# A decoder step in three-term float32: GpSimd splits one half chunk of weights at each hand-over, and four weight tiles start from the first x tile

## What is computed

```python
x = x + 0.5 * rms_norm(swiglu(rms_norm(x, ng[0]), ffn1_gate[l], ffn1_up[l], ffn1_down[l]), ng[1])
mix, s, cg, cs = mixer(rms_norm(x, ng[2]), cache_gdn_conv[l], cache_sconv[l], state_gdn[l], segments, ...)
x = x + rms_norm(mix, ng[3])
x = x + 0.5 * rms_norm(swiglu(rms_norm(x, ng[4]), ffn2_gate[l], ffn2_up[l], ffn2_down[l]), ng[5])
```

## Time and profile before

| | |
|---|---|
| median of 3 runs | 1414.64 us (1412.66 to 1418.47) |
| the profiled execution | 1414.16 us, of which the span of its instructions is 1412.4 us |
| TensorE busy | 1391.3 us, 99% |
| VectorE busy | 862.0 us, 61% |
| ScalarE busy | 629.7 us, 45% |
| GpSimd busy | 32.4 us, 2% |
| mean granted TensorE clock | 0.994 of full speed |

### The profile page before, as it was taken

The page is one execution under the profiler, slowest core; times in us unless marked ns, Lnnn a source line. Parts: engine busy times, 40 slices in busy tenths (PEclk is TensorE's granted clock), DMA queues, the critical chain, the costliest instruction groups (busy, mean ns, idle before and its releaser), DMA issues.

```text
span 1412.4 us, 25251 instructions
## 1 busy us (share of the span) xinstructions
PE 1391.3 (99%) x10788; PEld 1369.1 (97%) x10788; DVE 862.0 (61%) x1510; ACT 629.7 (45%) x1002; POOL 32.4 (2%) x130
## 2 busy tenths in 40 slices
PE   9999999999999999999999999999999999999997
PEld 8999999898999999999999999998999999999997
DVE  5655533787697765553376555337886968655433
ACT  5443333582644544433354333335826345444331
POOL 0000000110000000000000000001100000000000
PEclk9999999999999999999999999999999999999998
DMA  6544344422216334434435443444221263444342
GB/s 220 208 149 149 121 143 141 132 90 87 71 61 217 118 130 142 149 122 144 155 121 207 150 149 117 140 142 140 90 93 65 90 214 122 150 149 149 123 144 99
DMA packets 49760, 190.93 MB, mean 135 GB/s; under 512 B 6160, under 2 KB 8720, under 8 KB 49136
## 3 DMA queue, kind: packets, MB, share of 16 engines
q1 hardware_dynamic: 49040, 184.19, 38.9%
q0 software_dynamic: 608, 5.12, 0.9%
HBM read 182.86 MB, written 6.43 MB: 134 GB/s over the span
## 4 chain that ended last, share of the span: by engine, by line
PE 95%; DVE 3%; ACT 1%; issue 0%; DMA 0%; SPq 0%
PE PS L1493 27%; PE PS L1494 27%; PE PS L1495 27%; PE PS L1533 2%; PE PS L1664 2%; PE PS L1538 2%; PE PS L1534 2%; DVE WL L1040 1%; PE PS L1813 1%; PE PS L1662 1%; PE PS L1705 1%; ACT XH L751 1%; DVE XL L1052 1%; PE PS L1769 1%; PE PS L1788 1%; DVE X L1104 0%
## 5 line engine op out<-in xcount | busy, mean ns | idle before, releaser
L1493 PE MATMUL PS<-XH,WH 128*128 128x336 f32 (+1 forms) x1728 | 550.6, 319 | 0.0
L1495 PE MATMUL PS<-XH,WL 128*128 128x336 f32 (+1 forms) x1728 | 543.2, 314 | 0.0
L1494 PE MATMUL PS<-XL,WH 128*128 128x336 f32 (+1 forms) x1728 | 542.8, 314 | 0.0
L1040 DVE TENSOR_TENSOR WL<-RAW,WH 128x1024 fp32r<-128x1024 f32 (+1 forms) x312 | 398.8, 1302 | 193.3 <-ACT WH L734 192.8
L734 ACT ACTIVATE WH<-RAW 128x1024 fp32r<-128x1024 f32 (+1 forms) x312 | 343.1, 1118 | 222.0 <-DMA RAW<-in_w_down 173.3
L1493 PEld LDWEIGHTS PS<-XH,WH 128*128 128x128 f32 x1728 | 325.4, 188 | 1.4 <-issue 0.4
L1494 PEld LDWEIGHTS PS<-XL,WH 128*128 128x128 f32 x1728 | 325.5, 188 | 0.3
L1495 PEld LDWEIGHTS PS<-XH,WL 128*128 128x128 f32 x1728 | 325.2, 188 | 0.0
L1493 PE MATMUL PS<-HH,WH 128*128 128x336 f32 (+1 forms) x704 | 221.4, 314 | 0.0
L1494 PE MATMUL PS<-HL,WH 128*128 128x336 f32 (+1 forms) x704 | 221.3, 314 | 0.0
L1495 PE MATMUL PS<-HH,WL 128*128 128x336 f32 (+1 forms) x704 | 221.2, 314 | 0.0
(11 more groups left out here) (252 smaller groups left out, 1220.7 us busy)
## 6 DMA issues: line engine op xcount, KB each, us to landing
RAW<-in_w_up SPq DMA_DIRECT2D x176, 512.0 KB, 4.3
RAW<-in_w_down SPq DMA_DIRECT2D x64, 704.0 KB, 4.1
RAW<-in_w_in SPq DMA_DIRECT2D x56, 512.0 KB, 4.3
RAW<-in_w_out SPq DMA_DIRECT2D x16, 512.0 KB, 4.2
SEQ_S<-in_states SPq DMA_DIRECT2D x2, 2048.0 KB, 9.7
out_state_s<-SEQ_S POOLq DMA_DIRECT2D x2, 2048.0 KB, 8.9
X<-in_x SPq DMA_DIRECT2D x8, 168.0 KB, 4.8
out_y<-X SPq DMA_DIRECT2D x4, 320.0 KB, 2.3
```

The lines of the kernel that those rows point to most:

```text
L1040: dve.tensor_tensor(WL[slot][:, cols], RAW[slot][:, cols], WH[slot][:, cols].bitcast(F32), ALU.subtract).then_inc(split_lo.sem, 1)
L1493: pe.matmul(out, wh, xh, start=first, stop=False)
L1494: pe.matmul(out, wh, xl, start=False, stop=False)
L1495: return pe.matmul(out, wl, xh, start=False, stop=last)
```

## The change

Five things change.

1. GpSimd makes the low part of the second half of the second chunk of each sub-layer (`second_half_low`, `POOL_SPLIT`). VectorE leaves it out, at the five hand-overs and at the start of the kernel. It counts in a semaphore of its own, `pool_lo`, and `LOW_PIECE` counts what is left for VectorE.
2. `entry` uses all four tiles from x tile 0 on. It waits for `pool_lo` ahead of the first matmul of `up2`.
3. In the FFN to mixer hand-over VectorE splits the half chunk first and `W8X` behind it.
4. `keep_busy` ahead of the spreading is two fillers everywhere; it was four at `j` 0 and 2.
5. GpSimd's split for the mixer stands ahead of its memsets and copies of `EXT` and `UEXT` in its queue; those for the next FFN and the next layer stand behind its DMAs.

```diff
+POOL_SPLIT = [c + 1 for c in FIRST_CHUNK]
+            def second_half_low(layer, j):
+                if layer == DEPTH:
+                    return
+                c = POOL_SPLIT[j]
+                slot, cols = slot_of(layer, c), piece(c, 1)
+                pool.wait_ge(split_hi.sem, split_hi.at(PIECE[c] + 1, layer))
+                pool.tensor_tensor(WL[slot][:, cols], RAW[slot][:, cols], WH[slot][:, cols].bitcast(F32),
+                                   ALU.subtract).then_inc(pool_lo.sem, 1)
+            second_half_low(0, 0)
             pool.wait_ge(in_hist, 32)
             for layer in range(DEPTH):
-
+                second_half_low(layer, 1)
                 pool.wait_ge(y_sq.sem, y_sq.at(KT - 1, layer))
...
                 pool.dma_start(io["state_s"][layer], SEQ_S[:, :, :, :]).then_inc(states_out.sem, 16)
+                second_half_low(layer, 2)
+                second_half_low(layer + 1, 0)
...
                 split_low(*second, 0)
+                if j == 0:
+                    dve.wait_ge(w8_hi.sem, w8_hi.at(0, layer))
+                    dve.tensor_tensor(W8X[:, :, 2 * HEADS:], W8R[:, :].rearrange("p (k c) -> p k c", k=KT),
+                                      W8X[:, :, 0:2 * HEADS].bitcast(F32), ALU.subtract).then_inc(w8_lo.sem, 1)
                 dve.wait_ge(y_root.sem, y_root.at(j, layer))
...
-                    if m == 2:
-                        split_low(*second, 1)
...
                     for slot, half in tiles:
+                        if kt == 0 and (slot, half) == (1, 1):
+                            split(layer, at + 1, 1)
...
-                for kt in range(2):
-                    part(kt, gate, up, gate2)
-                part(2, gate, up, gate2)
-                split(layer, at + 1, 1)
-                for kt in range(3):
-                    part(kt, up2)
-                part(3, gate, up, gate2, up2)
-                part(4, gate, up)
-                part(4, gate2)
-                part(5, gate, up)
-                part(4, up2)
-                part(6, gate, up)
-                part(5, gate2)
-                part(7, gate, up)
-                part(5, up2)
-                part(6, gate2, up2)
-                part(7, gate2, up2)
+                for kt in range(KT - 1):
+                    part(kt, gate, up, gate2, up2)
+                part(KT - 1, gate, up)
+                part(KT - 1, gate2, up2)
...
-                    keep_busy(2 if j == 1 else 4)
+                    keep_busy(2)
```

More of the change, by code:

```diff
@@ L94 @@
 PIECE = list(itertools.accumulate([2 if c in HALVED else 1 for c in range(CHUNKS)], initial=0))
+POOL_SPLIT = [c + 1 for c in FIRST_CHUNK]
+LOW_PIECE = list(itertools.accumulate([1 if c in POOL_SPLIT or c not in HALVED else 2 for c in range(CHUNKS)], initial=0))
 def end_of_chunk(c):
@@ L386, in decoder_trunk @@
         w8_hi, w8_lo = sig("w8_hi", 1), sig("w8_lo", 1)
-        split_hi, split_lo = sig("split_hi", PIECE[-1]), sig("split_lo", PIECE[-1])
+        split_hi, split_lo, pool_lo = sig("split_hi", PIECE[-1]), sig("split_lo", LOW_PIECE[-1]), sig("pool_lo", 3)
         products, first_cols = sig("products", PRODUCTS), sig("first_cols", 2)
@@ L1468, in _ @@
             split_low(0, 1, 0)
-            split_low(0, 1, 1)
             split_low(0, 2, 0)
@@ L1477, in _ @@
                 ffn(layer, 0)
-                dve.wait_ge(w8_hi.sem, w8_hi.at(0, layer))
-                dve.tensor_tensor(W8X[:, :, 2 * HEADS:], W8R[:, :].rearrange("p (k c) -> p k c", k=KT),
-                                  W8X[:, :, 0:2 * HEADS].bitcast(F32), ALU.subtract).then_inc(w8_lo.sem, 1)
                 boundary(layer, 0)
@@ L1501, in split @@
             def split(layer, c, half):
-                pe.wait_ge(split_lo.sem, split_lo.at(PIECE[c] + half, layer))
+                if half == 1 and c in POOL_SPLIT:
+                    pe.wait_ge(pool_lo.sem, pool_lo.at(POOL_SPLIT.index(c), layer))
+                else:
+                    pe.wait_ge(split_lo.sem, split_lo.at(LOW_PIECE[c] + half, layer))
             def x_tile(kt, n):
@@ L1551, in entry @@
                         part(kt, gate, up)
+                    split(layer, at + 1, 0)
                     for tile in (gate2, up2):
-                        split(layer, at + 1, tile[1])
                         for kt in range(KT):
```

## The result

The changed kernel takes **1419.54 us** (median of 11 runs, 1417.66 to 1424.87), the one before 1414.64 (11 runs, 1412.66 to 1418.47). The ratio is 1.0043, with an interval of 1.0031 to 1.0055: slower by 0.43%, just inside the half per cent that the prediction called no change, and 3.5 us above its number. The profiled execution took 1419.54 us with a span of 1417.8.

What follows compares the result with a forecast made beforehand. TensorE, busy 99% of the span, was taken as the bound. Later entries of 6.83 us less 5.30 gained gave +1.53 on the profiled 1414.16, stated as 1416 us; its own range was 1410 to 1421, the whole range 1406.5 to 1421.

Steps and rivals of the forecast that it cites:

- The hold, both ways: At each hand-over GpSimd's split, first to read SBUF, blocks VectorE's first addition until it ends: entries later by 6.83 us.
- Rival 1: At the hand-overs GpSimd, when first, shuts nobody out and additions stay on time: 1407.4 us, chance 0.25.
- Rival 2: At the hand-overs GpSimd and VectorE both slow each other a little: about 1411 us, chance 0.08.
- GpSimd's split: Low part of the half chunk, 1024 columns on GpSimd: taken as 2.1 us, between bounds of 1.0 and 3.1.
- The gain of the entry: In the five entries, four tiles from x tile 0 on end TensorE's waiting at each tile: 5.30 us less.
- The reciprocal's 1.44 us: Earlier reciprocal or spreading at three hand-overs, 0.58 us twice and 0.28, but swallowed because the addition waits for GpSimd.
- The late reload: SyncE reloads the slot of `gate` and `up` products 1.38 us later against the entry's end; covered, 0.27 us to spare.
- rival 4: Longer TensorE stands at the hand-overs drop the clock at each entry, 5 x 1.6 us: 1423.7 us, chance 0.07.
- Rival 3: GpSimd's first tensor_tensor, at the kernel's start, is late from loading; 3 us of waiting once: 1419 us, chance 0.08.

Runs made afterwards that it cites:

- e2: Kernel before, nothing moved, plus a GpSimd tensor_tensor of 128 x 936 on a scratch tile where the change puts its split, nobody waiting for it: 1417.97 us.
- e3: Kernel before, nothing moved, plus three GpSimd memsets of 128 x 936, which read nothing, where the change puts its split: 1413.80 us.
- e9: Changed kernel with GpSimd's split of 1024 columns cut into four instructions of 256 columns, semaphore raised by the last: 1412.34 us.
- e5: Changed kernel with ScalarE's high part of the half chunk made ahead of the last output tile, so GpSimd splits early: 1410.19 us.
- e4: Kernel before with only the half chunk split ahead of `W8X` and two fillers ahead of the spreading everywhere; no GpSimd split: 1414.39 us.
- e8: Changed kernel run once more, unaltered, for a second profile: 1420.92 us.
- e1: Changed kernel with 15 fillers behind the spreading where it had 7: 1420.25 us.
- e11: Kernel before without the seven fillers behind the spreading, nothing else altered: 1422.93 us.
- e12: Changed kernel with 15 fillers behind the spreading in place of 7, measured a second time: 1421.03 us.
- e6: Changed kernel with the high half made early, VectorE splitting both low halves ahead of its reciprocal and GpSimd none: 1410.67 us.
- e7: Changed kernel with high half early and both low halves on VectorE, but the three-tile entry of the kernel before: 1412.20 us.

## Why the prediction was right, and where it was off

- **The hold, both ways, is the mechanism.** L1123 for x tile 0 was to be about 2.2 us long; it is 2.36, 2.29 and 2.29 at the first three hand-overs, e2 shows the same hold without the change, e3 that it goes without the read, and e9 that it shortens with the pieces. Rival 1 is wrong by its own mark, the addition that "stays at 0.5". Rival 2 too: it is a full stop and no mutual slowing, since GpSimd's split takes the same 2.34 us where it holds an addition and where it holds nothing (e5, third hand-over).
- **GpSimd's split was mis-sized**: 2.35 us for 2.1. The entries were to start later by 1.05, 1.65, 1.43, 1.05 and 1.65 (6.83) and start later by 1.26, 1.79, 1.55, 1.19 and 1.80 (7.59). The estimate of 2.25 us from the Trainium skill ("GPSIMD Engine Reference", Elementwise side-by-side cycle accounting, its 4497 ns for 2048 columns halved) was nearer than my middle of two bounds; by it the sum would have been 1.53 + 0.75 = +2.3.
- **The gain of the entry** was 5.30 and was 5.4: 14.65 us at full clock for 14.68, 14.00 for 14.04. Hold and entry together are +2.2 in the hand-overs of the profile, +2.6 in the means less the clock.
- **The reciprocal's 1.44 us** were real, 1.3 in e4, and swallowed by the hold as said.
- **The late reload was costed at nothing with 0.27 us of spare; in one of two profiles it was short, and cost 0.4 us.** Against the entry's end SyncE issued it 1.39 us later (0.58 us ahead of the end, where it was 1.97), as worked out with 1.38; but from issue to ScalarE's start 4.37 us passed where 3.71 had. In e8, the same program, 3.30 us passed and nothing waited, so the spare is within what the transfer varies by. What lengthened it was not tried.
- **The clock is the term that was missing.** I gave rival 4 five falls of 1.6 us or none, and a chance of 0.07. Its price is right (1.55) and its trigger too (e1, e11, e12); it comes at three hand-overs in five. The argument against it was that in none of the entries before did the clock fall; but TensorE stood only 0.3 to 0.4 us ahead of them, and that row could not speak for 2.1 us of standing. A chance of each stand, summed, would have added 3 x 1.55 = 4.7 us to the profile's number; the rough split of the means has 3.6.
- **Rival 3**: the first GpSimd split ran at 15.35 for 2.50 us with nothing waiting for it, so no loading falls on the first use; its start lies within a VectorE split that ends at 15.58, and it is only 0.15 us longer than the others. The 6 us that the Trainium skill, "GPSIMD Engine Reference", Instruction dispatch, has for a first call of freshly loaded code are not seen there.

The miss in the number is +3.5 us. For the profile it can be told term by term: 1419.54 against 1414.16 + 1.53 = 1415.69 is +3.85, of which 0.76 are the later starts (7.59 - 6.83), -0.1 the entries, +4.65 the three falls, +0.4 the reload, and -1.9 the mixers, the start and the end, which vary between executions. So the mechanism held as forecast, and the direction with it, but that the time stayed within the stated range is in part luck: the range was made from GpSimd's bounds alone, and with falls at all five hand-overs, as in e11, another 3.1 us would have put it above 1421. Open stays why e1 and e12, clean in their entries, come near 1415 us in only four runs of fifteen, and what brings on the 10-us falls in the mixers, which e2, e6, e7 and e11 show in their profiles as well.

## What to carry to other kernels

Before work is moved to GpSimd, look at what VectorE does in that stretch: if it has two SBUF inputs and GpSimd's operation reads SBUF, the two take turns by whole instructions, and the one that comes second waits for the end of the other's. Move such work to where VectorE is idle or takes one input from PSUM (L1117 keeps its 0.56 us beside GpSimd's split), or cut it in short instructions; here the gain (0.23 to 0.27%) came from the operand made earlier together with the new order, and GpSimd was not needed for it. A stand of TensorE of 2 us can cost more than its length: count the clock's fall behind it as a chance with a price, and take that price from a stretch at the lower level.

## What the runs showed of the hardware

- The hold works per instruction and in either direction: additions of 0.51 us took 2.3 behind 1024 columns on GpSimd, 1.18 to 1.70 in e2, 0.74 behind 256 columns; pieces of 0.73 us took 1.00 behind VectorE. Behind GpSimd's end the addition needs another 0.36 us, less than its whole 0.51, and the split of `W8X` in e5 another 0.08 of its 0.23: 0.15 us less in both.
- GpSimd's subtraction takes 2.35 us for 1024 columns, 0.73 for 256, and 1.75 for 936 where both inputs and the output are one tile: the last is 1.87 ns a column, the first 2.29.
- The clock's falls last 3.4, 6.8 or 10.2 us and come and go between executions of one kernel: the changed one had them at hand-overs 2, 4 and 5 and then at 1, 4 and 5.
- Ahead of the entries TensorE stood 1.9 to 2.2 us in 15 cases (the changed kernel twice, e11), and a fall came at 11 of them; it stood 1.0 to 1.5 us in the five of e2's profile, and none came; nor in any entry behind a stand of 0.3 to 0.6 us.
